# Down projections of a two-block transformer: 14 of 76 weight units computed as 2x2 blocks with seven block products

## What is computed

```python
def swiglu(x, w_gate, w_up, w_down):            # D_FF = 2816
    return (jax.nn.silu(x @ w_gate) * (x @ w_up)) @ w_down
...
h = h + 0.5 * swiglu(rmsnorm(h, ffn1_norm[l]), ffn1_w_gate[l], ffn1_w_up[l], ffn1_w_down[l])
...
h = h + 0.5 * swiglu(rmsnorm(h, ffn2_norm[l]), ffn2_w_gate[l], ffn2_w_up[l], ffn2_w_down[l])
...
ff = jnp.square(jax.nn.relu(x @ w_ff1[l])) @ w_ff2[l]    # 1024 -> 4096 -> 1024
x = layer_norm(DEEPNORM_ALPHA * x + ff, ln2_g[l], ln2_b[l])
```

## Time and profile before

| | us |
|---|---|
| median of 3 runs | 2044.28 (2043.98 to 2044.53) |
| span of the profiled execution, first to last instruction | 2042.5 |
| TensorE busy | 2034.5, 10364 matmuls, granted clock 1.000 |
| VectorE busy | 1389.1 (68%) |
| ScalarE busy | 1018.4 (50%) |
| GpSimd busy | 92.8 (5%) |

### The profile page before, as it was taken

One profiled execution on the slowest core, in us unless ns is written; L12 is line 12 of the kernel. 1 busy time (PEld: TensorE's weight loads), 2 busy tenths in 40 slices (PEclk: granted clock), 3 DMA queues, 4 the chain that ended last, 5 costly groups with the idle time before them and its releaser, 6 DMA issues.

```text
span 2042.5 us, 25162 instructions
## 1 busy us (share of the span) xinstructions
PE 2034.5 (100%) x10364; PEld 1718.3 (84%) x10364; DVE 1389.1 (68%) x1624; ACT 1018.4 (50%) x1290; POOL 92.8 (5%) x133
## 2 busy tenths in 40 slices
PE   9999999999999999999999999999999999999998
PEld 7888888888888888888888888888888888888887
DVE  6655687775757566877675667757767677577675
ACT  6444576453445335775443365644444466445331
POOL 1001010000010001100100000000100000000000
PEclk9999999999999999999999999999999999999999
DMA  9655554465566656544656474555755656455552
GB/s 333 211 187 166 178 162 141 167 214 185 186 197 210 194 168 201 165 145 145 226 191 197 153 242 155 166 172 173 239 186 189 204 153 194 156 185 193 196 189 83
DMA packets 225569, 377.73 MB, mean 185 GB/s; under 512 B 6592, under 2 KB 113216, under 8 KB 225456
## 3 DMA queue, kind: packets, MB, share of 16 engines
q1 hardware_dynamic: 221472, 362.64, 54.1%
q0 software_dynamic: 3984, 13.49, 2.2%
HBM read 375.05 MB, written 1.05 MB: 184 GB/s over the span
## 4 chain that ended last, share of the span: by engine, by line
PE 98%; DVE 1%; ACT 0%; issue 0%; DVEq 0%; POOL 0%; ACTq 0%; POOLq 0%
PE pb L1656 63%; PE pb L1667 18%; PE pb L1670 9%; PE pb L1679 2%; PE pb L1725 1%; PE pb L1803 1%; DVE wl L2109 0%; PE pb L1802 0%; PE pb L1790 0%; PE pb L1860 0%; PE pb L1782 0%; PE pb L1645 0%; DVE lS L2292 0%; PE pb L1649 0%; PE pb L1647 0%; PE pb L1684 0%
## 5 line engine op out<-in xcount | busy, mean ns | idle before, releaser
L1891 ACT ACTIVATE wh<-raw 128x2048 fp32r<-128x2048 f32 (+2 forms) x347 | 654.2, 1886 | 626.6 <-PE pb L1656 271.3
L2109 DVE TENSOR_TENSOR wl<-raw,wh 128x2048 fp32r<-128x2048 f32 (+2 forms) x347 | 777.3, 2247 | 149.0 <-ACT wh L1891 147.8
L1656 PE MATMUL pb<-wh,x 128*128 128x512 f32 (+1 forms) x2144 | 651.3, 385 | 0.0
L1656 PEld LDWEIGHTS pb<-wh,x 128*128 128x128 f32 x2144 | 400.7, 188 | 77.9
L1656 PE MATMUL pb<-wl,x 128*128 128x512 f32 (+1 forms) x1072 | 421.1, 393 | 0.1
L1667 PE MATMUL pb<-x,wh 128*128 128x512 f32 x1568 | 397.0, 395 | 0.0
L1667 PEld LDWEIGHTS pb<-x,wh 128*128 128x128 f32 x1568 | 283.3, 189 | 51.8
L1656 PE MATMUL pb<-wl,mh 128*128 128x512 f32 (+1 forms) x740 | 255.7, 391 | 0.0
L1656 PE MATMUL pb<-wh,ml 128*128 128x512 f32 (+1 forms) x740 | 253.7, 388 | 0.0
L1656 PE MATMUL pb<-wh,mh 128*128 128x512 f32 (+1 forms) x740 | 253.5, 388 | 0.0
L1656 PEld LDWEIGHTS pb<-wl,x 128*128 128x128 f32 x1072 | 201.4, 188 | 42.2 <-issue 3.7
(11 more groups left out here) (365 smaller groups left out, 1611.8 us busy)
## 6 DMA issues: line engine op xcount, KB each, us to landing
raw<-in_w_in_dram SPq DMA_DIRECT2D x100, 1024.0 KB, 5.3
raw<-in_w_ff_dram SPq DMA_DIRECT2D x64, 1024.0 KB, 5.3
raw<-in_ffn_w_down_dram SPq DMA_DIRECT2D x44, 1024.0 KB, 4.9
raw<-in_ffn_w_up_dram SPq DMA_DIRECT2D x42, 1024.0 KB, 5.3
raw<-in_ffn_w_gate_dram SPq DMA_DIRECT2D x41, 1024.0 KB, 5.3
raw<-in_w_branch_dram SPq DMA_DIRECT2D x24, 1024.0 KB, 5.0
raw<-in_w_out_dram SPq DMA_DIRECT2D x16, 1024.0 KB, 5.0
raw<-in_w_in_dram SPq DMA_DIRECT2D x4, 832.0 KB, 4.4
```

Of the source, the lines that this page charges most:

```text
L1656: ins = e.matmul(pb[b][:, 0:c1 - c0], x[:, s, cols], w[:, n, c0:c1], start=(it["first"] and n == 0 and q == 0), stop=(it["stop"] and n == ...
L1891: e.activation(hi, raw, ACT.Copy).then_inc(m.high_done, 1)
L2109: e.tensor_tensor(lo, raw, hi.bitcast(F32), ALU.subtract).then_inc(m.low_done, 1)
```

## The change

**Seven products.** In 14 down units (units 2 and 3 of the first block in three of the four gated parts; D1, D2, E0 and E1 in both layers of the second stack) the product of the 2x2 blocks (two token halves by two slots) and (two slots by two column halves) is computed with seven block products where the usual way has eight. Each block product is three matmuls of 512 columns, so a unit has 21 matmuls and no longer 24. The products need four sums of weight blocks (`sum`) and four differences of hidden blocks (`diff`), each with a high part by ScalarE and a low part by VectorE. GpSimd makes the sums (three instructions, 1024, 512 and 512 elements a partition) and the differences (256, 128 and 128). Four of the seven products gather over the two units in the side banks 4 to 7; afterwards one ScalarE copy and eight VectorE instructions (`recombine`) take them into `h` and free the banks. The low part of a seven-unit waits for its sums, since it overwrites `raw`. One quarter of its weights is no longer split (1536 elements in two instructions).

**Relu on ScalarE.** `wrelu` becomes two ScalarE instructions, Relu and Square.

**Loads.** The small loads for the next mixer are put into the list before the last down group of a part, no longer at its start.

```diff
         elif k == "high":
...
-            e.activation(hi, raw, ACT.Copy).then_inc(m.high_done, 1)
+            if n is None:
+                e.activation(hi, raw, ACT.Copy).then_inc(m.high_done, 1)
+            else:
+                e.activation(hi[:, 0:512], raw[:, 0:512], ACT.Copy)
+                e.activation(hi[:, 1024:2048], raw[:, 1024:2048], ACT.Copy).then_inc(m.high_done, 1)
+        elif k == "sumhigh":
+            a.wait_ge(m.sums_ready, n + 1)
+            a.pe(it["after"])
+            e.activation(m.sumh[n % 2][:, :, :], m.sum[n % 2][:, :, :], ACT.Copy).then_inc(m.sum_high, 1)
...
+        elif k == "wrelu":
+            q = it["q"]
+            a.emptied(use)
+            e.activation(m.sg[q][:, :], m.sg[q][:, :], ACT.Relu).then_inc(m.rectified, 1)
+            a.ready(it["free"])
+            a.wait_ge(m.rectified, n + 1)
+            e.activation(m.mn[q][:, :], m.sg[q][:, :], ACT.Square).then_inc(m.product, 1)
```

```diff
+        elif k == "sums":
+            j, n = it["j"], it["n"]
+            B, V = m.raw[j % NL][:, :].rearrange("p (a n) -> p a n", n=512), m.sum[n % 2]
+            po.pe(it["after"])
+            po.pe(it["war"])
+            po.wait_ge(m.raw_landed[j % NL], 16 * ((j - 8) // NL + 1))
+            po.step(e.tensor_tensor(V[:, 0:2, :], B[:, 0:4:3, :], B[:, 1:2, :].broadcast_to([P, 2, 512]), ALU.add))
+            po.own_steps()
+            po.step(e.tensor_tensor(V[:, 2, :], V[:, 0, :], B[:, 3, :], ALU.add))
+            po.own_steps()
+            e.tensor_tensor(V[:, 3, :], V[:, 2, :], B[:, 2, :], ALU.add).then_inc(m.sums_ready, 1)
...
+            pe.wait_ge(m.low_done, it["j"] + 1)
+            pe.all_ready(it["need"])
+            for x, y, k, (b, g), first, stop in (
+                    ([x[:, s0, T] for x in a], w, 0, q1, begin, it["end"]),
+                    ([x[:, s1, T] for x in a], w, 2, q2, b2, False),
+                    ([x[:, 3, :] for x in d], w, 3, q3, b3, False),
+                    ([x[:, 1, :] for x in d], v, 0, q5, begin, it["end"]),
+                    ([x[:, 0, :] for x in d], v, 1, q7, begin, it["end"]),
+                    ([x[:, 2, :] for x in d], v, 2, q6, begin, it["end"]),
+                    ([x[:, s1, U] for x in a], v, 3, q4, b4, False)):
...
+                e.matmul(pb[b][:, :], x[0], y[1][:, k, :], start=first, stop=False)
+                e.matmul(pb[b][:, :], x[0], y[0][:, k, :], start=False, stop=False)
+                ins = e.matmul(pb[b][:, :], x[1], y[0][:, k, :], start=False, stop=stop)
...
+        elif k == "recombine":
+            q1, q5, q6, q7 = it["uses"]
...
+            e.tensor_tensor(E, Q6, W, ALU.add).then_inc(m.evac[q6[0]], 1)
+            e.scalar_tensor_tensor(h[0][0], Q1, c, h[0][0], ALU.mult, ALU.add).then_inc(m.evac[q1[0]], 1)
+            v.emptied(q6)
+            v.step(e.tensor_tensor(W, E, Q5, ALU.add))
+            v.step(e.tensor_tensor(V, E, Q7, ALU.subtract))
+            v.own_steps()
+            e.tensor_tensor(E, V, Q5, ALU.add).then_inc(m.evac[q5[0]], 1)
+            e.scalar_tensor_tensor(h[0][1], W, c, h[0][1], ALU.mult, ALU.add).then_inc(m.recombined, 1)
+            e.scalar_tensor_tensor(h[1][0], V, -c, h[1][0], ALU.mult, ALU.add).then_inc(m.recombined, 1)
+            v.emptied(q5)
+            e.scalar_tensor_tensor(h[1][1], E, c, h[1][1], ALU.mult, ALU.add).then_inc(m.evac[q7[0]], 1)
```

More of the change, by code:

```diff
@@ L446, in advance @@
         while self.nlo < self.nhi:
-            self.add("low", j=self.nlo)
+            n = self.seven.get(self.nlo)
+            self.add("low", j=self.nlo, n=n)
             self.nlo += 1
+            self.sum_low_next()
+            if n is not None:
+                self.sum_high_due = n
         while self.nhi < self.total and (self.nhi < NH or self.nhi - NH in self.freed) and self.nhi - self.nlo < most:
@@ L452, in advance, with sum_high_next, sum_low_next @@
             j = self.nhi
+            if self.seven.get(j, 0) > 1 and self.seven[j] - 2 not in self.sum_free:
+                break
             if j < 8:
                 self.x_split(j)
-            self.add("high", j=j, after=self.freed.get(j - NH))
+            n = self.seven.get(j)
+            if n is not None:
+                self.add("sums", j=j, n=n, after=self.freed[j - NH], war=self.sum_free.get(n - 2))
+            self.add("high", j=j, after=self.freed.get(j - NH), n=n)
             self.nhi += 1
+            self.sum_high_next()
+    def sum_high_next(self):
+        n, self.sum_high_due = self.sum_high_due, None
+        if n is not None:
+            self.add("sumhigh", n=n, after=self.sum_free.get(n - 2))
+            self.sum_low_due = n
+    def sum_low_next(self):
+        n, self.sum_low_due = self.sum_low_due, None
+        if n is not None:
+            self.add("sumlow", n=n)
     def x_split(self, s):
@@ L538, in group @@
             need = self.need(X, slots, [t])
-            if job["first"]:
-                for b, _, _ in job["segs"]:
+            if job.get("seven"):
+                if t == 0:
+                    self.seven_products(j, job)
+                self.tick()
+                continue
+            first = []
+            for b, _, _ in job["segs"]:
+                first.append((t, b) not in self.opened if job["first"] is None else job["first"])
+                if first[-1]:
                     self.main_use[t, b] = self.use(2 * t + b)
+                    self.opened.add((t, b))
             segs = [(self.main_use[t, b], c0, c1) for b, c0, c1 in job["segs"]]
@@ L671, in to_ln, with down @@
         return after
-    def down(self, name, l, k0, n_units, sizes, coef, after, end=False):
+    def down(self, name, l, k0, n_units, sizes, coef, after, end=False, loads=None):
         def epi(t, p, uses):
@@ L692, in cut, with seven @@
                 after(1, 1)
+        def seven(i):
+            return ("first" if i == min(self.seven_units) else "next") if i in self.seven_units else None
         u = 0
+        self.opened = set()
         for size in sizes:
-            first, last = u == 0, u + size == n_units
+            last = u + size == n_units
+            if last and loads:
+                loads()
             if last and after:
@@ L705, in down @@
                                  slots=[2 * (u + i), 2 * (u + i) + 1], segs=[(0, 0, 512), (1, 512, 1024)],
-                                 first=first and i == 0, last=last and i == size - 1, epi=epi)
+                                 first=None, last=last and i == size - 1, epi=epi, coef=coef,
+                                 seven=seven(u + i), end=u + i == max(self.seven_units, default=None))
                             for i in range(size)])
@@ L724, in ffn1 @@
             self.clear("M", range(12))
+            self.seven_units = () if opening or n0 else (2, 3)
             slot, c0 = 0, n0
@@ L747, in ffn1 @@
                 c0 += n
-            self.down(dn, l, n0, sum(chunks) // 256, sizes, 0.5, after if n0 else None)
+            self.down(dn, l, n0, sum(chunks) // 256, sizes, 0.5, after if n0 else None, loads=loads if n0 else None)
     def silu_t(self, n, root):
@@ L851, in split_into, with differences, high, low @@
         return ("split_low", n + 1)
+    def differences(self, q, need):
+        n = self.next("diff")
+        self.add("diff", q=q, n=n, need=need, after=self.sum_free.get(n - 2))
+        def high():
+            self.add("diffhigh", n=n, after=self.sum_free.get(n - 2))
+            self.later.append(low)
+        def low():
+            self.add("difflow", n=n)
+            self.ready["D", n, 0] = ("diff_low", n + 1)
+        self.later.append(lambda: self.later.append(high))
+        return ("diff_ready", n + 1)
     def ffn2(self, l, after, loads):
         self.mix_to_ffn()
-        if loads:
-            loads()
         for n0, n_chunks, sizes in ((0, 3, (2, 4)), (1536, 2, (2, 2)), (2560, 3, (2, 4))):
             self.clear("M", range(12))
+            self.seven_units = {0: (), 1536: (1, 2), 2560: (0, 1)}[n0]
             first = 2 if n0 == 0 else 0
@@ L870, in ffn2 @@
                     n_t += 1
-            self.down("w_ff2_2", l, n0, n_chunks * 2, sizes, 1.0, after if n0 == 2560 else None, n0 == 2560 and l == L - 1)
+            self.down("w_ff2_2", l, n0, n_chunks * 2, sizes, 1.0, after if n0 == 2560 else None, n0 == 2560 and l == L - 1,
+                      loads if n0 == 2560 else None)
     def start(self):
```

146 lines of the change are left out of this document (123 added, 23 removed).

## The result

| | before | after |
|---|---|---|
| median of 4 runs, us | 2044.4 (2043.98 to 2044.63) | 2096.55 (2095.52 to 2097.0) |
| span of the profiled execution, us | 2042.5 | 2093.7 |
| mean granted clock of TensorE | 1.000 | 0.988 |

The ratio is 1.0255 (95% interval 1.0241 to 1.027): the change costs 52 us, 2.6%. The sign was forecast, the size was not: 2096.55 lies above the range of 2054 to 2089.

The account below looks back on a forecast made before the run. TensorE's path was taken as the bound, with VectorE's order nearly late. From 2044.3 us, -9.5 + 17.4 + 6.0 + 10.4 + 5.7 + 3.6 = +33.6 gave 2077.9 us, 1.6% slower; range 2054 to 2089.

Parts of the forecast that it names:

- D1, both layers: Second stack's middle block: TensorE waits for `diffl` before this seven-unit, 8.7 us in each layer, +17.4 (13.2 to 19.2).
- V0, both layers: Wide unit after the middle block: TensorE waits for recombination to free bank 4, +2.1 and +3.9, together +6.0 us.
- E0, first layer: Last block's first seven-unit: bank 7 freed 7.9 us late, plus 2.5 for waits on sums, +10.4 us.
- E0, second layer: Last block's first seven-unit: late at its start and again for bank 7 at its sixth product, +5.7 us (3.3 to 8.4).
- clock: TensorE's granted clock falls to half in the longer waits: +3.6 us, the middle between nothing and 7.2.
- the gated parts at nothing: Gated parts: two down units (10.9 us) cover the recombination's 9.35, and sums and differences cost nothing.
- the loop through ScalarE: Per wide unit: reduction, Relu, Square, high copy and low part take 6.1 us against TensorE's 5.59.
- both orders of bank 4's release: Recombination before V0: bank 4 comes fifth in the first layer (+2.1 us), eighth in the second (+3.9 us).
- Rival A: Whole kernel: the slack holds and nothing waits, 2034.8 us; decided by `diffl` at D1 by 1524.95; chance 0.08.
- Rival D: Gated parts wait too: VectorE loses 2.5 us at each of six units, 15 more, about 2093 us; chance 0.03.
- the low part was not lengthened ... So I let GpSimd give way: Where GpSimd's sums meet VectorE's low parts: GpSimd yields, and VectorE later waits for it at the low part.
- The sum would move by under 2 us: If the port's first starter blocks the other, delay falls on VectorE's small instructions and the forecast total moves under 2 us.

## Why the prediction was too low

| step | predicted | measured |
|---|---|---|
| 42 matmuls | -9.5 | -8.7 |
| D1, both layers | +17.4 | +21.1 |
| V0, both layers | +6.0 | +7.15 |
| E0, first layer | +10.4 | +12.3 |
| E0, second layer | +5.7 | +5.8 |
| clock | +3.6 | +10.6 |
| in no term | | +3.0 |
| span | +33.6 | +51.2 |

Of the 17.6 us between the two sums the clock has 7.0, D1 3.7, E0 2.0, V0 1.2, the matmuls 0.8, and 3.0 were in no term.

**What held.** TensorE's path as the bound, the four places, who is late at each, the gated parts at nothing, the sums' price where nothing meets them (5.0 taken, 5.1 measured), the loop through ScalarE (D1 waits 2.0 us less without it), both orders of bank 4's release. E0 of the second layer is near by luck: the forecast had 2.9 before its first product and 2.8 before its sixth, measured are 5.31 and 0.46. Rival A fell at its own test: D1 started at 1533, not by 1526. Rival D fell with the gated parts' clean list of waits, though its 2093 came nearest, by another sum.

**The first step that failed: "the low part was not lengthened ... So I let GpSimd give way".** One meeting, in which a VectorE instruction began 0.45 us after GpSimd's and went through at 2.28, was made a rule for all. In the changed kernel VectorE loses 2.2 us in one instruction at 1506.31, and the run in which GpSimd works for nobody shows the same with no data between them. The Trainium skill (SBUF — State Buffer, on the two separate sides) says that whichever starts first keeps the shared port pair for its whole instruction while the other fully blocks. The 3.43 us agree with it, where I had said that the row contradicts it, and so do the 3.75 us of the sum that began inside a low part. Rows 11 look like this second case: GpSimd's 0.74 become 3.34 and end 0.6 us after the low part. But there GpSimd's record began 0.45 us ahead of the low part. That such a record can begin before GpSimd works the 3.75 and the 1.52 us show; what held GpSimd up in those 0.45 us stays open.

"The sum would move by under 2 us" was wrong too. The forecast held 9.1 us for the sums (4.2 at D1, 2.5 and 2.4 at E0), and leaving them out gave 15.3, some 6 more. At W1 the step can be seen by itself: by the forecast's walk (in the after trace 2.4 us earlier, as D1 is wanted at 1522.6) W1's reduction should have ended at 1508.1, and it ended at 1510.3, late by the 2.2 us of that one instruction. At D1 the forecast is 1.8 us short.

**The second: "The clock ... Taken: +3.6, the middle".** Its lower bound was nothing, it took half of 2.4 us a wait, and it counted three waits. The windows of the changed kernel show half clock behind all five waits of 4.5 us and more, at 1.6 to 2.9 us each and 10.6 in all. This is the largest single miss, and the run with extra matmuls, which got 5.6 us back, shows that it is the clock's. The upper bound's 2.4 a wait was near that, though its ground was not: the 4.8 us of the tail are one case of falls that came 2.0 to 5.0 us into a wait, and once only after one of 4.51. Between "nothing" and a figure reckoned from a row, the middle had no reason of its own.

**The third is a size:** a matmul of a seven-unit takes 0.230 us and not 0.227, 0.8 us over all. Why was not looked into. And the relu's own cost in the first blocks, 1.1 us here, had no term.
